# Seven block products for eight in the first SwiGLU too, and the modulation pieces spread over three SwiGLUs

## The reference

```python
def _swiglu(h, w_in, w_out):                  # w_in 1024 x 5632, w_out 2816 x 1024
    gt, up = jnp.split(h @ w_in, 2, axis=-1)
    return (jax.nn.silu(gt) * up) @ w_out

for i in range(DEPTH):                        # DEPTH = 2
    mods = (c_act @ ada_w[i] + ada_b[i]).reshape(B, 3, 3, D_MODEL)
    h = _modulate(x, norm_g[i, 0], mods[:, 0, 0], mods[:, 0, 1])
    x = x + MACARON_W * mods[:, 0, 2][:, None, :] * _swiglu(h, ffn_w_in[i, 0], ffn_w_out[i, 0])
    ...                                       # a mixer: MLA in stack layer 0, RWKV in layer 1
    h = _modulate(x, norm_g[i, 2], mods[:, 2, 0], mods[:, 2, 1])
    x = x + MACARON_W * mods[:, 2, 2][:, None, :] * _swiglu(h, ffn_w_in[i, 1], ffn_w_out[i, 1])
```

## Time and profile before

| | us |
|---|---|
| median of 3 runs | 2575.8 (2574.26 to 2576.21) |
| the profiled execution: device time | 2577.6 |
| its span, first to last instruction | 2575.8 |
| PE busy | 2187.2 (85%) |
| DVE busy | 1011.1 (39%) |
| ACT busy | 345.7 (13%) |
| mean DMA rate | 276 GB/s |

### The profile page before, as it was taken

The page is one execution under the profiler, slowest core; times in us unless marked ns, Lnnn a source line. Parts: engine busy times, 40 slices in busy tenths (PEclk is TensorE's granted clock), DMA queues, the critical chain, the costliest instruction groups (busy, mean ns, idle before and its releaser), DMA issues.

```text
span 2575.8 us, 36347 instructions
## 1 busy us (share of the span) xinstructions
PE 2187.2 (85%) x16127; PEld 1556.1 (60%) x16127; DVE 1011.1 (39%) x1895; ACT 345.7 (13%) x699; POOL 17.5 (1%) x21
## 2 busy tenths in 40 slices
PE   7999989999999999999999999976565666666666
PEld 5888768998999789889887878721111111111111
DVE  5554747667866575544454239410000000000000
ACT  3101331001000332111012211300000000000000
POOL 2000000000000000000000000000000000000000
PEclk9999999999999999999999999998888888778878
DMA  9999216676576240044332212799999999999998
GB/s 402 365 373 373 111 66 261 253 286 246 225 286 274 106 149 12 13 174 178 139 156 98 82 66 110 320 427 427 427 428 427 427 427 427 427 427 428 427 427 347
DMA packets 70851, 709.99 MB, mean 276 GB/s; under 512 B 7856, under 2 KB 7984, under 8 KB 9520
## 3 DMA queue, kind: packets, MB, share of 16 engines
q1 hardware_dynamic: 70704, 707.79, 67.0%
HBM read 706.71 MB, written 1.05 MB: 275 GB/s over the span
## 4 chain that ended last, share of the span: by engine, by line
PE 61%; DMA 25%; DVE 7%; issue 3%; another core or an unknown queue 2%; ACT 2%; SPq 0%; DVEq 0%; ACTq 0%
DMA arena<-in_experts 15%; PE ps L903 14%; PE ps L891 8%; PE ps L957 6%; PE ps L1306 4%; PE ps L1093 4%; DMA ring<-in_experts 4%; PE ps L818 3%; PE ps L825 3%; PE ps L835 3%; PE ps L1538 2%; PE ps L1574 2%; DMA hT_sq<-in_experts 2%; DMA xT<-in_experts 2%
## 5 line engine op out<-in xcount | busy, mean ns | idle before, releaser
L1538 PE MATMUL ps<-arena 128*32 128x512 f32 x1104 | 166.8, 737 | 103.3 <-DMA arena<-in_experts 102.7
L1624 ACT ACTIVATE arena<-ps 128x256 f32<-128x256 f32 (+6 forms) x206 | 110.9, 546 | 991.3 <-PE ps L1552 314.9
L2108 DVE CUSTOM_DVE_ANT_0 hT_sq<-arena 128x1024 f32<-128x1024 f32 x184 | 215.3, 1220 | 0.6 <-DVE dots L2108 0.2
L1538 PEld LDWEIGHTS ps<-arena 128*32 128x32 f32 x1104 | 33.5, 123 | 226.8 <-DMA arena<-in_experts 157.0
L903 PE MATMUL ps<-xT,arena 128*128 128x128 f32 x1280 | 155.4, 278 | 2.8 <-DVE arena L2191 2.8
L903 PEld LDWEIGHTS ps<-xT,arena 128*128 128x128 f32 x1280 | 150.4, 195 | 3.0 <-DVE arena L2191 3.0
L1574 PE MATMUL ps<-arena 128*32 128x512 f32 x608 | 98.8, 775 | 55.7 <-DMA arena<-in_experts 52.9
L2705 DVE TENSOR_TENSOR arena<-arena,ps 128x512 f32<-128x512 f32 x16 | 11.0, 687 | 293.1 <-issue 218.8
L2712 DVE TENSOR_TENSOR arena<-ps,arena 128x512 f32<-128x512 f32 x16 | 11.1, 691 | 289.3 <-PE ps L1574 289.3
L903 PE MATMUL ps<-hT_sq,arena 128*128 128x128 f32 x960 | 117.5, 276 | 2.0 <-DVE hid L2086 2.0
L903 PEld LDWEIGHTS ps<-hT_sq,arena 128*128 128x128 f32 x960 | 115.5, 192 | 4.4 <-issue 2.3
(11 more groups left out here) (447 smaller groups left out, 3231.7 us busy)
## 6 DMA issues: line engine op xcount, KB each, us to landing
arena<-in_experts SPq DMA_DIRECT2D x106, 2048.0 KB, 50.2
arena<-in_ada SPq DMA_DIRECT2D x96, 1024.0 KB, 11.6
ring<-in_experts SPq DMA_DIRECT2D x34, 2048.0 KB, 50.1
ring<-in_ring_w SPq DMA_DIRECT2D x51, 1024.0 KB, 5.1
arena<-in_ffn_blocks SPq DMA_DIRECT2D x46, 1024.0 KB, 7.8
arena<-in_ffn_down SPq DMA_DIRECT2D x42, 1024.0 KB, 5.0
con<-in_experts SPq DMA_DIRECT2D x17, 2048.0 KB, 50.4
hT_sq<-in_experts SPq DMA_DIRECT2D x17, 2048.0 KB, 50.1
```

Of the source, the lines that this page charges most:

```text
L1538: last = mm(ps[32 * n:32 * n + 32, part, :], e_xe[:, kt, :], w[:, (kt % 2) * SLOT + n * 512:(kt % 2) * SLOT + (n + 1) * 512], start=kt == ...
L1624: return f(dst, src, ACT.Copy)
L2108: nc.vector.tensor_tensor_reduce(buf[:, out_at * D:(out_at + 1) * D], w, c_rows[:, which * D:(which + 1) * D], 1.0, 0.0, ALU.mult, ALU.add ...
```

## The change

SwiGLU 0 gets the blocked form of the others, and its plain code is gone. The pieces are spread by a table: three to a group over SwiGLUs 0, 1 and 2, with less at the edges. So SwiGLU 0 has 31 pieces (before 40 and 4 under MLA), SwiGLU 1 has 29 and SwiGLU 2 has 28 (before 22 each). The third piece of a group goes to `fill(2)`, between the second group of weight sums and the next step of `quads`. The eight pieces of rounds 18 and 19 lie in groups 3 to 5 of SwiGLU 2 (before: the last group of SwiGLU 1 and the first three of SwiGLU 2). The first blocked group of every SwiGLU runs in another order: p2 and the first down half move ahead of the wait for `sums`, and `raw_hidden` is cut in two with the weight sums between. SP issues `down` of group 0 ahead of the pieces.

```diff
-BLOCKED = (1, 2, 3)
+BLOCKED = (0, 1, 2, 3)
+ADA_SPREAD = ((1, 3, 3, 3, 3, 3, 3, 3, 3, 3, 3), (1, 3, 3, 3, 3, 3, 3, 3, 3, 2, 2), (1, 2, 1, 3, 3, 3, 3, 3, 3, 3, 3))
...
-        FIRST_PRODUCTS = ("p1", "p5", "p6", "p2", "p7", "p4", "p3")
+        FIRST_PRODUCTS = ("p1", "p2", "p6", "p5", "p7", "p4", "p3")
...  SP
+            def other_groups(n, between=()):
+                t0, g0 = NG * n, LAST * n
+                for g in range(2):
+                    pieces(n, g)
+                for g in range(2, NG):
+                    if g == 2:
+                        sp.wait_ge(sem("gate_up_ready"), 2 * n + 3)
+                    else:
+                        sp.wait_ge(sem("products"), 7 * (g0 + g - 2))
+                    blocks(n, g)
+                    pieces(n, g)
+                    down(t0 + g - 1)
+                    if g in between:
+                        load(between.index(g))
...
-            for seq, lo, hi in ((0, 1, 4), (1, 4, 6), (2, 6, 8)):
-                ffn(lo, hi)
-                load(seq)
-            ffn(8, NG)
+            other_groups(0, (5, 7, 9))
...  PE, group(g)
                     if g == 1:
                         h_part(ready, KT - 1)
-                        pe.wait_ge(sem("hid_ready"), 2 * u0 + 1)
+                        pe.wait_ge(sem("hid_ready"), 2 * n + 1)
+                        product(g, 0, "b11", a11, first=True)
+                        pe.wait_ge(sem("quad_acts"), 5 * (g0 + g) - 4)
+                        product(g, 0, "b21", a12)
+                        down_half(0, 0)
+                        pe.wait_ge(sem("sums"), g0 + g)
+                        pe.wait_ge(sem("hid_ready"), 2 * n + 2)
+                        product(g, 1, "t2", s2, first=True)
+                        product(g, 6, "t1", s1, first=True)
...
-                    down_half(g - 1, 0)
+                    down_half(g - 1, int(g == 1))
...  DVE
+                if n == 0:
+                    hidden(0)
                 s_sums(ready)
+                if n > 0:
+                    raw_hidden(n, 0)
                 for i in range(4):
                     t_sum(n, 1, i)
-                raw_hidden(t0 - g0)
-                gate_of(site(n // 2, 2 if n % 2 else 0) + 16, 0.5)
+                if n > 0:
+                    raw_hidden(n, 1)
+                    gate_of(site(n // 2, 2 if n % 2 else 0) + 16, 0.5)
...
-                pieces(0, slice(0, 2))
+                pieces(0, slice(0, 3))
...
                         if i == 0:
                             pieces(g, slice(0, 1))
+                        elif i == 2:
+                            pieces(g, slice(1, -1))
                         elif i == 3:
-                            pieces(g, slice(1, 2))
+                            pieces(g, slice(max(1, len(ada_pieces(n, g)) - 1), None))
```

234 lines of the change are left out of this document (80 added, 154 removed).

## The result

The changed kernel takes **2582.67 us** (median of 9 runs, 2579.73 to 2585.04) against 2575.8 us for the kernel before in the same comparison (9 runs, 2574.26 to 2577.88): ratio 1.0027, 95% interval [1.0017, 1.0037]. It is slower, by 0.27%. The forecast was 2570.1 us, 0.2% faster, with a range that ended at 2581.0. Both the size and the sign were wrong.

What follows compares the result with a forecast made beforehand. PE was taken to bound SwiGLUs 0 and 1. Terms of -6.4, -0.5, +3.2 and -2.0 us for SwiGLUs 0 to 3 gave -5.7: 2577.6 to 2571.9 profiled, median 2570.1, range 2560.5 to 2581.

Steps and rivals of the forecast that it cites:

- The blocked form of SwiGLU 0: SwiGLU 0: blocked groups of 19.42 us replace plain ones of 20.72, 244.4 against 256.75, so -12.4 us.
- The MLA loads: SwiGLU 0: three loads between down and the weights of groups 6, 8 and 10 make PE idle, +5.0 us (3.0 to 7.4).
- the clock: SwiGLU 0: PE's clock falls after the two longer waits at the MLA loads, +1.0 us in all (0 to 3.3).
- L: Lateness of gate and up weights at DVE's weight sums: 0.7 us on average before, 0.8 taken, 3.3 with an MLA load.
- L - 0.9: Three-piece groups: delay a third piece gives all loads behind it once L passes 0.9 us; below that, none.
- c: Middle blocked group: the end of PE's product p7, from which times are counted; DVE begins weight sums at c + 1.1.
- slack of 2.3: Middle blocked group: sums ready at c + 10.0, needed by PE at c + 12.3, so 2.3 us to spare.
- SwiGLU 1: SwiGLU 1: new first-group order less a wait for sums, -1.0 us; third pieces' lateness +0.5 (0 to 5); together -0.5.
- SwiGLU 2: SwiGLU 2: first groups -6.8, four-pass pieces in groups 3 to 5 +8.2, clock +1.3, lateness +0.5; together +3.2 us.
- SwiGLU 3: SwiGLU 3: first group 20.8 us instead of 23.1, -2.3; clock after short copy waits +0.3; together -2.0 us.
- (b): Rival: MLA loads, clock and SwiGLU 2's pieces take the whole gain, -0.2 us, 2575.6 us; chance 0.24.
- (c): Rival: loads set the pace, each three-piece group adds 0.65 us, +12, 2587.9 us; decides from mean lateness 1.3; chance 0.11.

Runs made afterwards that it cites:

- e13: Kernel of e11 with each third piece issued behind the gate and up weights of the group after: 2555.13 us, ratio 0.9923 to the kernel before.
- e1: Changed kernel with the three MLA weight loads issued together after SwiGLU 0's last load: 2574.88 us, ratio 0.9993 to the kernel before.
- e12: Changed kernel with each third piece issued behind the next group's gate and up weights instead of ahead of down: 2571.15 us, ratio 0.9988 to the kernel before.
- e8: Changed kernel with the last piece of each SwiGLU 0 group from group 1 loaded only in 64 of 2048 columns: 2574.25 us, ratio 0.9992.
- e3: Kernel before with only the new order of the first blocked group in SwiGLUs 1 to 3: 2571.13 us, ratio 0.9982.
- e2: Changed kernel with SwiGLU 2's eight four-pass pieces spread two a group over groups 1 to 5: 2573.25 us, ratio 0.9991 to the kernel before.
- e6: Kernel of e5 with 24 more small matmuls on PE at the start, shifting the instruction stream: 2565.90 us, ratio 0.9965 to the kernel before.
- e10: Kernel before with 104 more matmuls of 32 columns on PE in its idle stretch at the start: 2580.49 us, ratio 1.0016.
- e5: Changed kernel with MLA loads behind SwiGLU 0's last load and two pieces a group in SwiGLU 2's groups 1 to 5: 2566.66 us, ratio 0.9958.
- e11: Kernel of e6 with ScalarE's early copy and one piece moved from SwiGLU 0's first blocked group to SwiGLU 2's group 5: 2562.16 us, ratio 0.9946.
- e7: Changed kernel with SP issuing the next group but one's gate and up weights ahead of down: 2593.57 us, ratio 1.0068 to the kernel before.

## Why the prediction was wrong

**The blocked form of SwiGLU 0, -12.4: right.** The group takes 19.41 (forecast 19.42), and with the third pieces behind the weights and the MLA loads late the stage is 12.8 shorter (e13; part of that may be its start, which is 1.4 later, and its one piece less). That the extra DVE work lies under PE held too. The first two groups took 0.8 more than forecast: 31.64 us from PE's 41.29 to the down half at 72.93, against 30.8.

**The MLA loads, +5.0 (bounds 3.0 to 7.4), and the clock, +1.0: here the forecast failed.** From the down half of group 2 at 72.93 to that of group 10 at 238.33 are 165.4 us, against 8 x 19.42 = 155.4: **+10.0** in place of 6.0. By group it is 1.2 in group 5, 4.4 with the clock's fall in group 6, 2.4 in 8 and 2.1 in 10; each wait costs some 0.26 more than its row says.

The step that failed is the lateness L with which the MLA loads were met, and with it the price of the third piece. The forecast took L = 0.8 from the kernel before, where down never has a piece just ahead of it, and gave the third pieces no term of their own in SwiGLU 0, though it had written that such a piece "delays all behind it by L - 0.9". In the changed kernel L (DVE's first weight sum, less c + 1.1) was 1.6, 1.8 and 3.3 in groups 2, 3 and 4, all before an MLA load could act. L - 0.9 was too small as well: in e1 down landed 1.6, 3.2, 3.6 and 2.4 us later than the 4.8 it takes alone, where L was 1.3, 2.5, 3.0 and 3.0 (forecast 0.4, 1.6, 2.1 and 2.1). So PE waited in group 5, for which no term stood, and in group 6 the MLA load came on top: L 5.1, a wait of 2.55 and the fall of the clock, where the forecast had 3.3 and 1.0. What was built on L held: the slack of 2.3 (L = 3.3 left a wait of 0.96), and the third piece's issue at c + 7.3 + L, to within 0.1.

There was a second step left out, a smaller one. When c + 7.3 + L passes c + 10.7, that is, when L passes 3.4, SP itself is late with down and all behind it, and the forecast did not ask for this. But 5.7 of the 10.0 us were lost by the down half at 156.26, before the first hold of more than 0.4 us could act (e12 lost 1.8 up to there). With the piece's bytes gone and holds of 0.8 to 1.2 us left the stretch costs 4.4 (e8), and with neither 4.0 (e12): within the forecast's 3.0 to 7.4 for the MLA loads alone. So the bytes ahead of down are shown as the cause of most of the difference; the share of the standing is small where it was tested, and for holds of 2 us it was not tested by itself.

**SwiGLU 1, -1.0 + 0.5: the second term was too small.** The order alone gives -1.6 (e3), third pieces bring it to +0.6, so they cost 2.2 and not 0.5 (bounds 0 and 5). With the third piece behind the weights they cost 0.2 (222.72 against 222.48). SP holds nothing back there (third piece at 452.66, down free at 453.1 and issued at 453.26), but L stood at 2.0 to 2.8 in five groups and down landed 6.4 us after its issue in the median, against 4.8 before: the same transfer ahead of down, by itself. The order was worth 0.6 more than its -1.0.

**SwiGLU 2, +3.2: it came to +3.1, in part by luck.** PE waits before the sums of groups 4, 5 and 6 were 1.38, 1.95 and 2.28 (forecast 1, 2.7, 3.1), with one fall of the clock. Its parts were each some 1 us too large, with opposite signs: with the four-pass pieces taken apart (e2) the stage is 5.3 shorter than before, against a forecast of 6.8 - 0.5 = 6.3, and those pieces with the clock cost 8.4 against 8.2 + 1.3 = 9.5. The order alone is worth -3.4 (e3); the rest of the -5.3 comes with fewer pieces in the first groups.

**SwiGLU 3, -2.0: -1.6.** The wait of 1.16 for the copy was forecast at 1.4. No fall of the clock followed it in any trace.

**The RWKV stage, 0: +2.4.** No term stood for it. PE stops there for 1.48 us and in smaller pieces, because more instructions ahead (5867 of PE's matmul records in place of 5394) put the short matmuls at another place in the stream. e6 and e10 show this from both sides. That it runs out of instructions is read from the instruction packets, which start again only shortly before the stop.

**The MLA stage, 0: +1.5, by chance as far as the traces tell.** PE idles 1.99 us ahead of L927 in every kernel, and in 6 of 15 traces (after, e5 to e8, e11) the ten matmuls behind it ran wholly or in part at the lower clock (3.5 to 4.1 us in place of 2.4). Kernels made from the changed one have it in some traces and not in others; the kernel before and the two made from it have it in none of three, too few to say that the change has no part in it.

**The rivals.** (b), in which the loads and the clock take it all, came nearest to the time, and (c), loads that set the pace, to the mechanism: its lateness from group to group is what was seen, and L was above its bound of 1.3 in most three-piece groups. But it is not the sum of the bytes that does it: with the same bytes in another order, e12 loses 4.0 us where the changed kernel loses 10.0. Of the 7.1 us from (b)'s 2575.6 to the result, 2.4 are RWKV and 1.5 MLA in the profiled execution, which stood in no case. The range ended 1.7 us too early, less than the 2.4 of RWKV; without these the time would have lain inside it by luck, with the step above as wrong as it is. The Trainium skill (DMA: Bandwidth & Descriptors, "Where 436 GB/s comes from") holds loads from HBM to some 358 GB/s, against 421 in the experts' rows of before and after; the 0.5 to 1.5 us that an MLA load still costs in e12 decide nothing between the two.

**Small waits, undercounted.** For e13 theory A said 0 to 2 us below e11, and it was 7.0. The profiled executions differ by 7.2: 1.6 in SwiGLU 0, 2.2 and 2.8 in SwiGLUs 1 and 2, 1.7 of clock in MLA, less a start 1.1 later. Each of the many waits of 0.3 to 0.6 us had been taken for what the sums cost anyway.

What stays open: why a piece just ahead of down delays it by 0.3 to 1.6 us more than L - 0.9, and why PE waited 3.6 us for down in some groups of e7 and not at all in others.

## What to carry to other kernels

When one in-order queue serves several buffers, ask of each load whether it can come to stand just ahead of one that is wanted sooner, and take the lateness from the kernel as it will be, not from the one before: a load whose issue moves with the lateness turns a small lateness into a standing one, and each further late load then costs in full. Look too whether the wait of one load can outlast the time when those queued behind it could go. Put the load with the most slack behind those that are wanted soon; here a third load per group then cost 0.2 us in SwiGLU 1 in place of 2.2. And before blaming a change for time lost in a stage that it does not touch, look there for idle time without a releaser: code added elsewhere moves the place at which a dense stretch runs short of instructions.
